# Attention scores of bundled blocks as 64x64 quarter products, with the value products between them and a semaphore wait on TensorE

## The reference

```python
h = rmsnorm(x, norm_g)
proj = einsum('bsd,de->bse', h, w_in) + b_in              # 2816 columns
q, k, v, z_a, u_s, v_s, z_s = split(proj)                 # 512,128,128,512,512,512,512
attn = banded_sink_attention(q, k, v, sinks) * silu(z_a)  # 8 query heads, 2 key heads, head 64
u_s, v_s = gelu(u_s), gelu(v_s)
sgu = u_s * (W_s @ layernorm(v_s) + b_s) * silu(z_s)      # causal 128x128 W_s, 8 groups
x = x + concat(attn, sgu) @ w_out + b_out
out = rmsnorm(x, final_norm_g)
```

## Time and profile before

| | us |
|---|---|
| median of 3 runs | 509.37 (508.74 to 510.1) |
| the profiled execution's own time | 509.76 |
| span of its slowest core | 508.1 (the eight cores: 505.2 to 508.1) |
| TensorE busy | 489.9 (96%) |
| ScalarE busy | 327.6 (64%) |
| VectorE busy | 319.9 (63%) |
| GpSimd busy | 178.2 (35%) |

### The profile page before, as it was taken

The page is one execution under the profiler, slowest core; times in us unless marked ns, Lnnn a source line. Parts: engine busy times, 40 slices in busy tenths (PEclk is TensorE's granted clock), DMA queues, the critical chain, the costliest instruction groups (busy, mean ns, idle before and its releaser), DMA issues.

```text
span 508.1 us, 10146 instructions; the slowest of 8 cores (505.2 to 508.1 us)
## 1 busy us (share of the span) xinstructions
PE 489.9 (96%) x3441; PEld 243.6 (48%) x3441; DVE 319.9 (63%) x475; ACT 327.6 (64%) x573; POOL 178.2 (35%) x219
## 2 busy tenths in 40 slices
PE   8798988999999999999999999999999999999994
PEld 3683454444544445444454445444454445444442
DVE  1679864726656357763786267663678547846775
ACT  3322967955685755966678467847658764737965
POOL 1103636501336132350345103361334833543132
PEclk9899999999999999999999999999999999999999
DMA  8999699292245912592327804386042504220115
GB/s 230 326 318 330 168 145 327 86 201 90 58 151 145 228 44 84 161 172 85 126 83 177 196 6 162 120 172 207 6 151 94 83 1 165 85 83 2 51 76 206
DMA packets 44403, 71.16 MB, mean 140 GB/s; under 512 B 27584, under 2 KB 27840, under 8 KB 44352
## 3 DMA queue, kind: packets, MB, share of 16 engines
q1 hardware_dynamic: 42912, 68.17, 45.9%
q0 software_dynamic: 1152, 2.10, 3.1%
q10 hardware_dynamic: 288, 0.24, 0.2%
HBM read 49.53 MB, written 16.78 MB: 131 GB/s over the span
## 4 chain that ended last, share of the span: by engine, by line
PE 80%; DMA 9%; ACT 3%; issue 2%; POOL 2%; DVE 2%; SPq 0%; ACTq 0%; DVEq 0%; POOLq 0%
PE pp L578 38%; PE pp L855 21%; PE pp L653 9%; DMA xe<-w_in 5%; PE pp L788 3%; PE pp L622 2%; DMA xa<-x 2%; PE pp L740 2%; DMA xT<-xn 2%; PE pp L783 2%; PE pp L745 1%; PE pp L698 1%; POOL st_ms L522 1%; DVE w_all L511 1%; POOL w_out_bf L961 1%
## 5 line engine op out<-in xcount | busy, mean ns | idle before, releaser
L578 PE MATMUL pp<-xT,w_all 128*128 128x512 bf16 x1056 | 236.2, 379 | 3.1 <-DVE w_all L511 1.5
L578 PEld LDWEIGHTS pp<-xT,w_all 128*128 128x128 bf16 x1056 | 101.5, 98 | 127.0 <-issue 7.1
L855 PE MATMUL pp<-w_out_bf,mixT 128*128 128x512 bf16 (+1 forms) x520 | 117.3, 376 | 0.0
L842 POOL TENSOR_TENSOR xe<-xe,bout_sb 128x1024 f32<-128x1024 f32 x28 | 67.1, 2399 | 64.1 <-DMA xe<-x 32.3
L855 PEld LDWEIGHTS pp<-w_out_bf,mixT 128*128 128x128 bf16 x520 | 48.9, 98 | 56.3 <-issue 0.6
L859 DVE TENSOR_TENSOR xe<-pp,xe 128x512 f32<-128x512 f32 x56 | 38.2, 686 | 29.0 <-PE pp L855 28.7
L751 ACT ACTIVATE PT<-pp 128x1536 bf16<-128x1536 f32 x32 | 46.3, 1447 | 13.8 <-PE pp L745 13.7
L653 PE MATMUL pp<-w_all,xT 128*128 128x512 bf16 x224 | 51.0, 379 | 0.0
L867 ACT ACTIVATE junk<-xe 128x1024 bf16<-128x1024 f32 x28 | 29.7, 1059 | 29.9 <-DVE xe L859 29.8
L660 ACT ACTIVATE vs_f<-vs_f 128x512 f32<-128x512 f32 x32 | 19.8, 624 | 36.7 <-DVE vs_f L658 33.7
L873 DVE SCALAR_TENSOR_TENSOR xe<-xe,st_fr,gf_sb 128x1024 f32<-128x1024 f32 x28 | 37.1, 1327 | 10.0 <-POOL st_fr L871 9.6
(11 more groups left out here) (87 smaller groups left out, 612.7 us busy)
## 6 DMA issues: line engine op xcount, KB each, us to landing
xa<-x SPq DMA_DIRECT2D x32, 512.0 KB, 8.2
xe<-x SPq DMA_DIRECT2D x28, 512.0 KB, 3.8
out<-xe SPq DMA_DIRECT2D x28, 512.0 KB, 2.7
xe<-w_in SPq DMA_DIRECT2D x12, 512.0 KB, 13.6
mixT<-w_in SPq DMA_DIRECT2D x10, 512.0 KB, 15.9
w_out_bf<-w_out POOLq DMA_DIRECT2D x8, 256.0 KB, 9.3
out<-w_all SPq DMA_DIRECT2D x4, 256.0 KB, 2.4
LR<-sgu_wT SPq DMA_DIRECT2D x1, 512.0 KB, 13.2
```

The lines of the kernel that those rows point to most:

```text
L578: ins = e.matmul(bank(h), lhsT=w_all[:, cb, k, :], rhs=xT[:, xb, k, :], start=(k == 0), stop=(k == 7))
L842: G.op("pool", lambda e: e.tensor_tensor(out=buf[:, s, :], in0=buf[:, s, :], in1=bout[:], op=ALU.add), reads=["c_bout"], writes=[key], cos ...
L855: ins = e.matmul(bank(h)[:, 0:width], lhsT=mixT[:, mb, ec, tt * 128:(tt + 1) * 128], rhs=w_out[:, ec, cols], start=(ec == 0), stop=(ec == 7))
```

## The change

In the 18 bundles the X and Y scores are computed like the Z scores, by matmuls with 64 x 64 weights: eight of them in place of the four row-mode ones. The four Z matmuls of the scores move behind the eight quad-mode value products. The value products become two operations, `mmz` (quad) and `mmxy` (col). The operation with the Z scores has a `fence`: a dependency on the operation with the X and Y scores that does get a semaphore wait, though both are on TensorE. A bundle is then: X and Y scores (8 quad), Z value products (8 quad), the wait, Z scores (4 quad), X and Y value products (8 col), mixing products (8 col). Scores outside the bundles keep their matmuls and their order. The planner's costs are now 0.24, 0.24, 0.12 and 0.43 for the four pieces, where they were 0.45 and 0.75; two new names, ("sc", p2) and ("pv", p2), tell it that the exponential waits for the Z scores and the logarithm for `mmxy`.

```diff
--- before.py
+++ after.py
@@ -75,13 +75,14 @@
 
 class Op:
     __slots__ = ("alts", "deps", "alloc", "uses", "prio", "phase", "gate", "mode", "dsem", "kb", "n", "left", "outs",
-                 "eng", "fn", "fin", "index", "dval", "nready", "final", "after", "port", "follow")
+                 "eng", "fn", "fin", "index", "dval", "nready", "final", "after", "port", "follow", "fence")
 
     def __init__(self):
         self.outs = []
         self.follow = []
         self.fin = None
         self.final = False
+        self.fence = None
 
 
 class Graph:
@@ -337,7 +338,7 @@
         for o in merged[e]:
             need = {}
             for d in o.deps:
-                if d.eng == "pe" and e == "pe":
+                if d.eng == "pe" and e == "pe" and d is not o.fence:
                     continue
                 sem, val = (d.dsem, d.dval) if d.dsem is not None else (eng_sem[d.eng], d.index)
                 if seen.get(id(sem), 0) >= val:
@@ -723,33 +724,46 @@
         def blk(i):
             return slice(i * 256, (i + 1) * 256)
 
-        def scores(n, lead=None):
+        def scores(n, between=None):
 
             st, j = n // 4, n % 4
             qb, p2, ph, v0 = st % 2, n % 2, 3 * st + PH_EXP, st + 0.1 * j
             h = Bank("S", 3)
             cur, prev = (st % 3) * 4 + j, ((n - 1) // 4 % 3) * 4 + (n - 1) % 4 if n else (st % 3) * 4 + j
 
+            def at(i):
+                return pp[:, h.at + i // 2, (i % 2) * 256:(i % 2 + 1) * 256]
+
+            def quads(e, sets):
+                for where, qk in sets:
+                    for kh, (qh, slot) in enumerate(qk):
+                        for g in range(2):
+                            r, c, q0 = slice(g * 64, (g + 1) * 64), slice(kh * 64, (kh + 1) * 64), j * 128 + qh * 64
+                            ins = e.matmul(at(where[g])[c], lhsT=kT[r, slot, c], rhs=qT[r, qb, :, q0:q0 + 64], start=True, stop=True,
+                                           skip_group_check=True)
+                return ins
+
+            whole = ((BLK_X, ((1, cur), (1, cur))), (BLK_Y, ((0, prev), (0, prev))))
+            rest = ((BLK_Z, ((0, cur), (1, prev))),)
+
             def mms(e):
-                def at(i):
-                    return pp[:, h.at + i // 2, (i % 2) * 256:(i % 2 + 1) * 256]
-
                 for where, slot, qh in ((BLK_X, cur, 1), (BLK_Y, prev, 0)):
                     for g in range(2):
                         r = slice(g * 64, (g + 1) * 64)
                         e.matmul(at(where[g]), lhsT=kT[r, slot, :], rhs=qT[r, qb, :, j * 128 + qh * 64:j * 128 + qh * 64 + 64],
                                  start=True, stop=True, skip_group_check=True)
-                for kh, slot in ((0, cur), (1, prev)):
-                    for g in range(2):
-                        r, c = slice(g * 64, (g + 1) * 64), slice(kh * 64, (kh + 1) * 64)
-                        ins = e.matmul(at(BLK_Z[g])[c], lhsT=kT[r, slot, c], rhs=qT[r, qb, :, j * 128 + kh * 64:j * 128 + kh * 64 + 64],
-                                       start=True, stop=True, skip_group_check=True)
-                return ins
+                return quads(e, rest)
             kn = {n // 4 % 3, max(n - 1, 0) // 4 % 3}
-            o = G.op("pe", mms, reads=[("qT", qb, c) for c in range(4)] + [("kT", k) for k in kn], cost=0.45, alloc=[h],
-                     prio=v0 - 10, mode=("row", "quad"), gate=ph, lead=lead)
+            need = [("qT", qb, c) for c in range(4)] + [("kT", k) for k in kn]
+            if between is None:
+                o = G.op("pe", mms, reads=need, writes=[("sc", p2)], cost=0.45, alloc=[h], prio=v0 - 10, mode=("row", "quad"), gate=ph)
+            else:
+                o = G.op("pe", lambda e: quads(e, whole), reads=need, writes=[("sc", p2)], cost=0.24, alloc=[h], prio=v0 - 10, mode="quad", gate=ph)
+                between(o)
+                z = G.op("pe", lambda e: quads(e, rest), reads=need, writes=[("sc", p2)], cost=0.12, uses=[h], prio=v0 - 10, mode="quad", lead=o)
+                z.fence = o
             G.op("act", lambda e: e.activation(out=PT[:, p2, :], in_=banks_of(h).rearrange("p a b -> p (a b)"), func=AF.Exp, scale=0.125),
-                 uses=[h], writes=[("PT", p2)], cost=1.47, prio=v0 - 0.5, phase=ph)
+                 uses=[h], reads=[("sc", p2)], writes=[("PT", p2)], cost=1.47, prio=v0 - 0.5, phase=ph)
 
             def mul(e):
                 v = PT[:, p2, :].rearrange("p (i c q) -> p i c q", i=6, c=4)
@@ -769,19 +783,22 @@
             hv = Bank("V", 2)
             cur, prev = (n // 4 % 3) * 4 + j, ((n - 1) // 4 % 3) * 4 + (n - 1) % 4
 
-            def mmpv(e):
-                def half(qh, what, g):
-                    return pp[g * 64:(g + 1) * 64, hv.at + qh, what * 256:(what + 1) * 256]
-
-                def weights(what, slot, r, g):
-                    return ones64[r, :] if what else v_r[r, slot, g * 64:(g + 1) * 64]
-
+            def half(qh, what, g):
+                return pp[g * 64:(g + 1) * 64, hv.at + qh, what * 256:(what + 1) * 256]
+
+            def weights(what, slot, r, g):
+                return ones64[r, :] if what else v_r[r, slot, g * 64:(g + 1) * 64]
+
+            def mmz(e):
                 for what in range(2):
                     for kh, slot in ((0, cur), (1, prev)) if n else ((0, cur),):
                         r = slice(kh * 64, (kh + 1) * 64)
                         for g in range(2):
-                            e.matmul(half(kh, what, g), lhsT=weights(what, slot, r, g), rhs=PT[r, p2, blk(BLK_Z[g])], start=what == 0,
-                                     stop=False, skip_group_check=True)
+                            ins = e.matmul(half(kh, what, g), lhsT=weights(what, slot, r, g), rhs=PT[r, p2, blk(BLK_Z[g])], start=what == 0,
+                                           stop=False, skip_group_check=True)
+                return ins
+
+            def mmxy(e):
                 for what in range(2):
                     for qh, where, slot in ((1, BLK_X, cur), (0, BLK_Y, prev)) if n else ((1, BLK_X, cur),):
                         for g in range(2):
@@ -789,16 +806,20 @@
                                            start=n == 0 and what == 0, stop=True, skip_group_check=True)
                 return ins
             kn = {n // 4 % 3, max(n - 1, 0) // 4 % 3}
-            G_op = dict(reads=[("PT", p2), "ones64"] + [("v", k) for k in kn], cost=0.75, alloc=[hv], mode=("quad", "col"))
-            if j < 3:
-                lead = scores(n + 1)
-                if st in SGU_ALONE:
-                    G.op("pe", mmpv, prio=v0 - 11, **G_op)
-                else:
-                    lead.prio = v0 - 11
-                    G.op("pe", mmpv, prio=v0 - 11, lead=lead, **G_op)
+            need = [("PT", p2), "ones64"] + [("v", k) for k in kn]
+
+            def pv_z(lead):
+                return G.op("pe", mmz, reads=need, writes=[("pv", p2)], cost=0.24, alloc=[hv], mode="quad", prio=v0 - 11, lead=lead)
+
+            lead = None
+            if j < 3 and st in SGU_ALONE:
+                scores(n + 1)
+            if j < 3 and st not in SGU_ALONE:
+                lead = scores(n + 1, pv_z)
+                lead.prio = v0 - 11
             else:
-                lead = G.op("pe", mmpv, prio=v0 - 11, **G_op)
+                lead = pv_z(None)
+            G.op("pe", mmxy, reads=need, writes=[("pv", p2)], cost=0.43, uses=[hv], mode="col", prio=v0 - 11, lead=lead)
             if st not in SGU_ALONE:
                 mix_mm(st, j, lead)
             lb = n % 2
@@ -808,7 +829,7 @@
                     ins = e.activation(out=LR[:, lb, c * 128:(c + 1) * 128].rearrange("p (h q) -> p h q", h=2),
                                        in_=banks_of(hv)[:, :, 256 + c * 64:256 + (c + 1) * 64], func=AF.Ln, bias=esink[:, c:c + 1])
                 return ins
-            G.op("act", lnop, uses=[hv], reads=["esink"], writes=[("LR", lb)], cost=1.05, prio=v0 - 0.6, phase=ph)
+            G.op("act", lnop, uses=[hv], reads=["esink", ("pv", p2)], writes=[("LR", lb)], cost=1.05, prio=v0 - 0.6, phase=ph)
             G.op("act", lambda e: e.activation(out=LR[:, lb, :], in_=LR[:, lb, :], func=AF.Exp, scale=-1.0), reads=[("LR", lb)],
                  writes=[("LR", lb)], cost=0.65, prio=v0 - 0.6, phase=ph)
             fz = lambda e: e.tensor_tensor(out=LR[:, lb, :].rearrange("p (c q) -> p c q", c=4),
```

## The result

The changed kernel takes 513.52 us (median of 6 runs, 512.61 to 514.4), the kernel before 509.55 beside it: ratio 1.0082, 95% interval 1.0069 to 1.0095. I had forecast 509.9 with a range to 512.0, and slower with a chance of 0.26. Timed again on another chip it is 511.88 against 508.17, ratio 1.0070 (1.0057 to 1.0084). It is slower, by 0.7 to 0.8%, or 3.7 to 4 us. Executions in which one die ran long at a lower clock are left out of all ratios and intervals, and of a median where they would move it.

The account below looks back on a forecast made before the run. TensorE, busy 96% of the span, was taken to bound the kernel. 18 bundles at +0.03 us gave +0.5 us, other terms zero: 509.9 us against the 509.37 median, with an 8-in-10 range of 507.7 to 512.0.

Parts of the forecast that it names:

- What bounds the kernel: TensorE, busy 96% of the span; gains or losses inside a bundle go one for one into the time.
- Quarter scores, 0.14 and 0.11: X and Y scores in a bundle become two quad steps, 0.14 and 0.11 us, their products running four abreast.
- Rival E: In the bundles, quarter products expose weight loads or don't run four abreast: +3.9 us, 513.8 us; chance 0.04.
- The wait, Z scores at 0.57: In a bundle, Z scores start 0.57 us after the first score, so TensorE stands 0.11 us for its own semaphore.
- Cold start, 0.23 with the change to col: Z scores behind the wait take 0.23 us including the mode change, against 0.21 warm.
- Bundle 1.27, +0.5 us: First score to first mixing product takes 1.27 us against 1.24: +0.03, times 18 bundles +0.5 us.
- a stall of at most 0.06: In a bundle, 50 to 100 ns semaphore reading would start Z scores at 0.47 to 0.52 us; not used.
- Rival B: The wait before the Z scores is nearly free: -1.9 us, 507.5 us; chance 0.12.
- The bundle without the wait: With no wait before the Z scores, a bundle takes 1.15 us, or 1.13 with finer steps of 0.107.
- The exponential's 0.25 hidden: The exponential starts 0.25 us later behind the Z scores, hidden by 2.8 us of room before the value products.
- The planner: I put 0 into the sum.: New costs and random shifts change the order from about 60 us on; booked as 0, the rest in the range.
- Rival C: New order brings a wait for the transposed input at a stage's start: +1.7 us, 511.6 us; chance 0.20.

Follow-up runs that it names:

- moving the loads away: Changed kernel with the next stage's input loads on SyncE's queue issued after all four transposing DMAs: ratio 1.0088 to the kernel before.
- the wait on Y: Changed bundles, Z scores waiting for all eight X and Y products, in the engine order of the kernel before: 508.91 us against 508.36, ratio 1.0011.
- the wait on X: Changed bundles in the engine order of the kernel before, Z scores waiting for the four X products alone: 507.01 us against 508.36, ratio 0.9972.

## Why the prediction was wrong

*What bounds the kernel*: right. After 86 us TensorE had no idle time but 0.67 us, on the slowest core alone, and with the order held each change of its work came through one for one: +0.6 in the stretch gave +0.56 in time, and -1.35 gave a ratio of 0.9972, or -1.4.

*Quarter scores, 0.14 and 0.11*: right, 0.133 and 0.11. They run four abreast. The Trainium skill's page "TensorE: Matmul & The Clock Gate", part "Packing small matmuls — row/col tiling", says that a weight load overlaps only with another row group's matmuls, though the same part also allows it for the background weight buffer. The trace shows no such limit: X, Y and the value products follow each other with fresh weights for both halves after 0.11. Rival E didn't come. Its 513.8 us is nearest to the measured time, and that is chance: the bundle is 1.27 and not 1.4.

*The wait, Z scores at 0.57*: right, 0.58. *Cold start, 0.23 with the change to col*: right, 0.23. *Bundle 1.27, +0.5 us*: right, 1.271 and +0.65 in the count of bundles, +0.56 in time with the order held. From the end of the last Y product to the Z scores it is 0.165, where I took 0.15 with bounds of 0.10 and 0.17. The estimate from the Trainium skill's page "Advanced Engine Details and Errata", section "Network/Comms" (a stall of at most 0.06), would have been wrong; it was 0.12. Rival B didn't come. (The bundle without the wait adds up to 1.14 with steps of 0.107, not 1.13.)

*The exponential's 0.25 hidden*: TensorE has no wait for it after 86 us in the changed kernel.

*The planner: I put 0 into the sum.* This is the step that failed. The new order costs 1.3 us in the stretch and 0.3 in the tail, on every core, measured alone as ratio 1.0036, 1.8 us. I had even written that there is nearly nothing to win there and something to lose, and then took the end of the range for the value. Rival C named the right place (the transposed input of stage 2) but the wrong mechanism for most of it: a typical core loses by one wait of 0.4 us, two halts of 0.2 and two more departures from full mode, none of which a view of the kernel before could name. Where the late input did come for 1.79 us, I had left out the lower clock behind it, 1.7 us on top of 1.8. That this brought the rest of the 3.7 to 4 us isn't shown: in the second timing the profiled execution had no late input on any core, and moving the loads away gained nothing.

*Outside the span*: not in the prediction. After the span's end 0.6 to 0.8 us more pass in the changed kernel than in before, and they go away with 40 idle instructions at the end of TensorE's program. So much is shown. Where TensorE's program ends may be what counts; but two kernels with as many instructions in it don't have the excess, and the cause stays open. The spread of the slowest core over the median one was 2.5 and 2.0 us in the two timings of the changed kernel and 1.1 to 1.5 in before. With the 40 instructions it was 1.4, so 0.5 to 1 us of the 3.7 to 4 are this spread. In the one profiled execution with a late input of 1.79 us, that input made the slowest core; whether the spread is more than chance in 5 or 6 runs is open. The parts then are 0.6 (bundles), 1.6 (order), 0.6 to 0.8 (excess) and 0.5 to 1 (spread); the cause of the last two isn't known.

## What to carry to other kernels

A fixed order written by a planner is part of the change whenever costs, or the number of operations, change: price it by emitting the new code in the old order, and don't book it at zero when the old order has no idle time left. A wait that replaces a change of mode wins only if it is fulfilled early: put it on the one product that conflicts, which here turned +0.6 into -1.4 us in the old order. And a price read from start to start in one island of the timeline can be right to 0.01 us while the total is off by over 3.

## What the runs showed of the hardware

A satisfied semaphore wait takes TensorE's sequencer about 0.1 us (64 at the head: 6.3 us; 162 at the end: 16.9 us from the last matmul to the span's end), so waits aren't free if many stand together. TensorE's own semaphore, from the start of the last of four quarter products to TensorE's next start, took 0.43 us with the wait on Y and 0.46 with the wait on X. From the product's listed end that is 0.165 in both, a little more than the 0.14 and 0.12 between TensorE and ScalarE in the earlier trace rows. The time between the last instruction and the end of the run isn't a constant: 1.5 to 1.8 us in eleven kernels, 1.8 to 3.2 in the changed one and two made from it.
